# FoX attention in groups of two key tiles, with the first pair's operands read in two parts

## What is computed

```python
qa, ka, va, za, qf, kf, vf, zf, ff, ga, gf = jnp.split(u @ w_in[i], split_idx, axis=-1)
y_swa = _swa_branch(qa, ka, va, sinks[i]) * jax.nn.silu(za)     # 8 heads, window 128 + 16 meta keys, sink logit
log_f = jax.nn.log_sigmoid(ff + b_forget[i])
y_fox = _fox_branch(qf, kf, vf, log_f) * jax.nn.silu(zf)        # 8 heads, causal over all keys
merged = (jax.nn.sigmoid(ga + b_gate[i, 0]) * (y_swa @ w_up_swa[i])
          + jax.nn.sigmoid(gf + b_gate[i, 1]) * (y_fox @ w_up_fox[i]))
h = h + _rmsnorm(merged @ w_out[i], g_post[i])
# _fox_branch, per head: softmax(q k * scale + c_q - c_k, causal) @ v, with c = cumsum(log_f)
```

## Time and profile before

| what | us |
|---|---|
| median of 3 runs (lowest, highest) | 869.65 (867.27, 871.06) |
| the profiled execution, its own time | 866.6 |
| its span in the profile | 864.8 |
| first FoX tile to the start of the tile x = 8 of the last pair | 504.9 to 657.6 |
| from there to the first matmul of the fourth stage | 657.6 to 678.1 |
| the fourth stage | 678.1 to 864.8 |

### The profile page before, as it was taken

How to read it: one execution, slowest core, us unless ns; L and a number is a source line. 1 busy time by engine, 2 the same in 40 slices (tenths; PEclk the granted TensorE clock), 3 DMA queues, 4 the chain that set the end, 5 groups by cost and what they waited for, 6 DMA issues and landing times.

```text
span 864.8 us, 12858 instructions
## 1 busy us (share of the span) xinstructions
PE 809.0 (94%) x4514; PEld 651.2 (75%) x4514; DVE 500.1 (58%) x1050; ACT 314.6 (36%) x637; POOL 348.1 (40%) x284
## 2 busy tenths in 40 slices
PE   3999989999999999999999959998988799999996
PEld 3999989887878878878878746656654578878885
DVE  7934886357677686565564627676777434442112
ACT  6431241333333323333333236565667022232111
POOL 3412322444445444434444025655557244412221
PEclk9999999999999999999999979999999799999999
DMA  9331424569964626636635799946500645533221
GB/s 285 106 116 51 124 68 129 124 171 261 242 176 145 171 86 185 172 98 181 158 113 130 185 233 247 256 124 172 124 1 2 212 131 147 143 127 125 97 91 73
DMA packets 120879, 124.99 MB, mean 145 GB/s; under 512 B 29824, under 2 KB 91344, under 8 KB 120816
## 3 DMA queue, kind: packets, MB, share of 16 engines
q1 hardware_dynamic: 119376, 119.92, 50.9%
q10 hardware_dynamic: 1440, 4.26, 1.3%
HBM read 90.93 MB, written 34.92 MB: 146 GB/s over the span
## 4 chain that ended last, share of the span: by engine, by line
PE 76%; DVE 9%; issue 4%; SPq 3%; DMA 3%; POOL 2%; ACT 2%; DVEq 0%; ACTq 0%; POOLq 0%
PE PS L1827 18%; PE PS L1828 18%; PE PS L1829 18%; PE PS L2063 3%; PE PS L2065 3%; PE PS L2064 3%; PE PS L1924 2%; PE PS L1984 2%; DVE t_val L1579 2%; PE PS L1964 1%; SPq L871 1%; PE PS L1965 1%; PE PS L2003 1%; DMA QBs<-q_dram 1%; POOL acc L1199 1%
## 5 line engine op out<-in xcount | busy, mean ns | idle before, releaser
L1130 POOL TENSOR_TENSOR ops<-s_sum,ops 128x512 fp32r<-128x512 f32 x64 | 87.4, 1376 | 114.1 <-ACT ops L1228 114.1
L1827 PE MATMUL PS<-t_hi,ops 128*128 128x512 f32 x256 | 101.1, 395 | 0.0
L1828 PE MATMUL PS<-t_lo,ops 128*128 128x512 f32 x256 | 99.8, 390 | 0.0
L1829 PE MATMUL PS<-t_hi,ops 128*128 128x512 f32 x256 | 99.8, 390 | 0.0
L1130 POOL TENSOR_TENSOR ops<-raw,ops 128x512 fp32r<-128x512 f32 x48 | 65.0, 1354 | 70.0 <-ACT ops L1228 69.9
L1199 POOL TENSOR_TENSOR acc<-acc,p_fox 128x400 f32<-128x400 f32 (+5 forms) x76 | 61.5, 830 | 2.5 <-ACT p_fox L1352 0.9
L1151 POOL TENSOR_TENSOR w_plain<-raw,w_plain 128x1024 fp32r<-128x1024 f32 x10 | 28.0, 2801 | 85.0 <-ACT w_plain L1257 85.0
L1658 DVE TENSOR_TENSOR z_tmp<-u,PS 128x512 f32<-128x512 f32 x48 | 33.0, 687 | 48.9 <-PE PS L1829 28.1
L1352 ACT ACTIVATE p_fox<-PS,neg_c_col 128x512 f32<-128x512 f32 (+5 forms) x112 | 54.1, 532 | 17.2 <-PE PS L1970 14.4
L1228 ACT ACTIVATE ops<-s_sum 128x512 fp32r<-128x512 f32 x64 | 39.6, 624 | 54.9 <-DVE s_sum L1460 41.1
L1829 PEld LDWEIGHTS PS<-t_hi,ops 128*128 128x128 f32 x256 | 48.1, 188 | 10.6
(11 more groups left out here) (203 smaller groups left out, 2192.1 us busy)
## 6 DMA issues: line engine op xcount, KB each, us to landing
raw<-in_w_in_dram SPq DMA_DIRECT2D x34, 512.0 KB, 5.2
q_dram<-stage_b SPq DMA_DIRECT2D x32, 256.0 KB, 3.0
g_dram<-stage_b SPq DMA_DIRECT2D x32, 256.0 KB, 2.0
tanh_g<-g_dram SPq DMA_DIRECT2D x16, 512.0 KB, 3.9
max_k<-k_dram SPq DMA_DIRECT2D x16, 260.0 KB, 5.3
max_c<-neg_c_dram SPq DMA_DIRECT2D x8, 520.0 KB, 6.0
KA<-k_dram SPq DMA_DIRECT2D x8, 520.0 KB
x_all<-in_x_dram SPq DMA_DIRECT2D x8, 512.0 KB, 8.1
```

The lines of the kernel that those rows point to most:

```text
L1130: nc.gpsimd.tensor_tensor(ops[:, i % OPS, 1], op_source(p, name), ops[:, i % OPS, 0].bitcast(F32), ALU.subtract).then_inc(op_ready, 1)
L1827: pe.matmul(dst, hi_w, hi, start=first, stop=False)
L1828: pe.matmul(dst, hi_w, lo, start=False, stop=False)
L1829: return pe.matmul(dst, lo_w, hi, start=False, stop=last)
```

## The change

The list is made of 28 groups of two tiles. A group is: the two tile steps; `norm` of the items scored in the group ahead; `score` of this group's items (32 items over the first 24 groups: one, one, two, one, one, two, ...); the values of both tiles of the group ahead; `exp`; closing steps; `pv_swa` of the items transposed in the group ahead; `trans` of the items normalised in this one. `den` and the first two `rec` come two groups after the group of a block's last tile, the other two `rec` and `fin` one group later. `p_fox` gets 8 buffers, `probs` 4, `S_RING` stays 3. The loads of pair 0 are cut: 11 loads with values of key tiles 0 to 4, queries 0 to 511 and keys 0 to 639 count on `fox_first`, for which the first tile waits; 12 more with the rest are issued between them and those of `v_a`, `v_b`, and are waited for at (0, 1, 0).

```diff
-PT_RING = 6
+PT_RING = 8
 PSWA_RING = 2
-PROB_RING = 3
+PROB_RING = 4
 ...
-    spread = len(units) - 8
-    next_item, unnormed, normed, untransposed, unvalued = 0, None, None, None, None
+    groups = len(units) // 2
+    spread = groups - 4
+    scored, transposed = [], []
     closing = []
-    for u, (j, q, i) in enumerate(units):
-        first, last = i == 0, i == 4 * q + 4
-        x = u % per
-        steps.append(dict(kind="tile", j=j, q=q, i=i, u=u, first=first, last=last))
-        if j + 1 < PAIRS:
-            for turn, what in ((1, "load_queries"), (2, "load_z"), (3, "load_keys"), (5, "load_values")):
-                if x == turn:
-                    steps.append(dict(kind=what, j=j + 1, u=u))
-        if (j, x) in ((0, 7), (0, 9)):
-            steps.append(dict(kind="load_up", d=(x - 7) // 2, u=u))
-        untransposed, normed = normed, unnormed
-        if unnormed is not None:
-            steps.append(item("norm", unnormed))
-            unnormed = None
-        slot = next_item < ITEMS and (u + 1) * ITEMS // spread > u * ITEMS // spread
-        if slot:
-            steps.append(score(next_item))
-        if u:
-            pj, pq, pi = units[u - 1]
-            steps.append(dict(kind="values", j=pj, q=pq, i=pi, u=u - 1, first=pi == 0, last=pi == 4 * pq + 4))
-        if slot:
-            steps.append(item("exp", next_item))
-            unnormed = next_item
-            next_item += 1
-        if closing and closing[0][0] <= u:
-            steps += closing.pop(0)[1]
-        if unvalued is not None:
-            steps.append(item("pv_swa", unvalued))
-            unvalued = None
-        if untransposed is not None:
-            steps.append(trans(untransposed))
-            unvalued = untransposed
-        if last:
-            closing.append((u + 2, [dict(kind="den", j=j, q=q)]))
-            closing.append((u + 3, [dict(kind="rec", j=j, q=q, c=c) for c in range(2)]))
-            closing.append((u + 4, [dict(kind="rec", j=j, q=q, c=c) for c in (2, 3)] + [dict(kind="fin", j=j, q=q)]))
-        if j == PAIRS - 1:
-            turn = {1: 0, 3: 1, 5: 2, 7: PAIRS + 2, 9: PAIRS - 1, 10: PAIRS, 11: PAIRS + 1}
-            if x in turn:
-                steps.append(dict(kind="split_y", s=turn[x], c0=0, c1=2))
-            if x == 12:
-                steps.append(dict(kind="split_y", s=2 * PAIRS - 1, c0=0, c1=1))
-            if x == 4:
-                steps.append(dict(kind="split_up", d=0))
-            if x == 8:
-                steps.append(dict(kind="split_up", d=1))
+    for g in range(groups + 1):
+        now = range(2 * g, 2 * g + 2) if g < groups else ()
+        for u in now:
+            j, q, i = units[u]
+            x = u % per
+            steps.append(dict(kind="tile", j=j, q=q, i=i, u=u, first=i == 0, last=i == 4 * q + 4))
+            if j + 1 < PAIRS:
+                for turn, what in ((1, "load_queries"), (2, "load_z"), (3, "load_keys"), (5, "load_values")):
+                    if x == turn:
+                        steps.append(dict(kind=what, j=j + 1, u=u))
+            if (j, x) in ((0, 7), (0, 9)):
+                steps.append(dict(kind="load_up", d=(x - 7) // 2, u=u))
+        for n in scored:
+            steps.append(item("norm", n))
+        turned, scored = scored, []
+        if g < spread:
+            scored = list(range(g * ITEMS // spread, (g + 1) * ITEMS // spread))
+        for n in scored:
+            steps.append(score(n))
+        for u in range(2 * g - 2, 2 * g) if g else ():
+            j, q, i = units[u]
+            steps.append(dict(kind="values", j=j, q=q, i=i, u=u, first=i == 0, last=i == 4 * q + 4))
+        for n in scored:
+            steps.append(item("exp", n))
+        due = [x for x in closing if x[0] <= g]
+        closing = [x for x in closing if x[0] > g]
+        for _, extra in due:
+            steps += extra
+        for n in transposed:
+            steps.append(item("pv_swa", n))
+        for n in turned:
+            steps.append(trans(n))
+        transposed = turned
+        for u in now:
+            j, q, i = units[u]
+            x = u % per
+            if i == 4 * q + 4 and g < groups - 1:
+                closing.append((g + 2, [dict(kind="den", j=j, q=q)] + [dict(kind="rec", j=j, q=q, c=c)
+                                                                       for c in range(2)]))
+                closing.append((g + 3, [dict(kind="rec", j=j, q=q, c=c) for c in (2, 3)] +
+                                [dict(kind="fin", j=j, q=q)]))
+            if j == PAIRS - 1:
+                turn = {1: 0, 3: 1, 5: 2, 7: PAIRS + 2, 9: PAIRS - 1, 10: PAIRS, 11: PAIRS + 1}
+                if x in turn:
+                    steps.append(dict(kind="split_y", s=turn[x], c0=0, c1=2))
 ...
+    steps += [dict(kind="den", j=j, q=q)] + [dict(kind="rec", j=j, q=q, c=c) for c in range(4)]
+    steps.append(dict(kind="fin", j=j, q=q))
 ...
                     elif (p, name) == (N_COUPLES - 1, "S2"):
                         sp.wait_ge(product_done, i + 1)
-                        load_values(sp, 0)
+                        load_values(sp, 0, fox_first, 0, 5)
                     elif (p, name) == (N_COUPLES - 1, "S1"):
                         sp.wait_ge(product_done, i + 1)
                         sp.wait_ge(halves_ready[0], 2)
                         sp.wait_ge(max_stored, 16 * PAIRS)
-                        load_queries_fox(sp, 0)
+                        load_queries_fox(sp, 0, fox_first, 0, 4)
                     elif (p, name) == (N_COUPLES - 1, "A12"):
-                        load_keys_fox(sp, 0)
+                        load_keys_fox(sp, 0, fox_first, 0, 5 * P)
+                        load_keys_fox(sp, 0, fox_loaded[0], 5 * P, LENGTH)
+                        load_queries_fox(sp, 0, fox_loaded[0], 4, NQ)
+                        load_values(sp, 0, fox_loaded[0], 5, NK)
                         sp.dma_start(v_a[0:A_ROWS, 0, :], vd[0, 0:A_ROWS]).then_inc(swa_loaded, 16)
 ...
-                    if i == 0 and q == 0:
+                    if (j, q, i) == (0, 0, 0):
+                        pe.wait_ge(fox_first, 16 * FIRST_LOADS)
+                        pe.wait_ge(halves_cleared, 3)
+                    elif i == 0 and q == (0 if j else 1):
                         pe.wait_ge(fox_loaded[j], 16 * FOX_LOADS)
 ...
-                                        p_fox[0:keys, x % PT_RING, 0:w], start=st["first"], stop=st["last"])
+                                        p_fox[x % PT_RING][0:keys, 0:w], start=st["first"], stop=st["last"])
```

More of the change, by code:

```diff
@@ L288, in attention_steps @@
     j, q, i = units[-1]
-    steps.append(dict(kind="values", j=j, q=q, i=i, u=len(units) - 1, first=False, last=True))
-    for _, extra in closing:
-        steps += extra
+    steps += [dict(kind="den", j=j, q=q)] + [dict(kind="rec", j=j, q=q, c=c) for c in range(4)]
+    steps.append(dict(kind="fin", j=j, q=q))
     steps.append(dict(kind="split_y", s=2 * PAIRS - 1, c0=1, c1=2))
-    assert next_item == ITEMS and unvalued is None and unnormed is None and untransposed is None and normed is None
+    assert not closing and not scored and not transposed
@@ L442, in build @@
         VF[1] = sb("VF1", [P, NK, P], on=ph2)
-        p_fox = sb("p_fox", [P, PT_RING, BANK], on=ph2)
+        p_fox = [sb(f"p_fox{n}", [P, BANK], on=ph2) for n in range(6)]
         sb("gap", [P, 64], on=ph2)
@@ L843, in natural, with load_queries_fox @@
             return PS[:, 2 * (n % 4):2 * (n % 4) + 2, :].rearrange("p a b -> p (a b)")
-        def load_queries_fox(queue, j):
-            n, done = j % 2, fox_loaded[j]
-            q_hi, q_lo = (qd[PAIRS + j, x] for x in range(2))
+        def load_queries_fox(queue, j, done, t0, t1):
+            n, cols = j % 2, slice(P * t0, P * t1)
+            q_hi, q_lo = (qd[PAIRS + j, x][:, cols] for x in range(2))
             for half in (Q0, Q1):
-                queue.dma_start(QA[n][half].bitcast(F32),
+                queue.dma_start(QA[n][half, :, cols].bitcast(F32),
@@ L858, in load_keys_fox @@
-        def load_keys_fox(queue, j):
-            n, done = j % 2, fox_loaded[j]
-            k_hi, k_lo = (kd[1 + j, x] for x in range(2))
+                queue.dma_start(QB[n][row:row + 1, h, cols].bitcast(F32),
+                                max_dram[2 * j + h, t0:t1].rearrange("(o t) q -> o (t q)", o=1)).then_inc(done, 16)
+        def load_keys_fox(queue, j, done, c0, c1):
+            n, cols = j % 2, slice(c0, c1)
+            k_hi, k_lo = (kd[1 + j, x][:, cols] for x in range(2))
             for half, src in ((Q0, k_hi), (Q1, k_lo)):
-                queue.dma_start(KA[n][half].bitcast(F32),
+                queue.dma_start(KA[n][half, :, cols].bitcast(F32),
@@ L1190, in _ @@
                         dst = acc[0:keys, f % 2, h, c0:c0 + w]
-                        tile = p_fox[0:keys, n % PT_RING, 0:w]
+                        tile = p_fox[n % PT_RING][0:keys, 0:w]
                         pool.wait_ge(fox_exp, n + 1)
```

44 lines of the change are left out of this document (27 added, 17 removed).

## The result

| what | before | after |
|---|---|---|
| median (lowest, highest), us | 870.36 (867.27, 872.48), 4 runs | 895.29 (893.75, 896.32), 4 runs |
| ratio, 95% interval | | 1.0288 [1.0252, 1.0324] |
| profiled execution, own time | 866.6 | 895.7 |
| span in the profile | 864.8 | 893.9 |
| first SWA `score` | 508.9 | 508.2 |

The change costs 25 us, where +8.7 us was forecast (877 named, range to 890): the sign was right and the time lies outside the range. In the two profiled executions the difference is 29.1 us, because the profiled one before lies 3.8 us under its median; attention alone has it all.

The account below looks back on a forecast made before the run. TensorE's own work plus short waits was taken to bound attention, with GpSimd setting its end. Terms -8.0 - 11.8 + 5.4 + 14.4 + 3.9 + 0.7 + 1.3 - 0.9 + 3.7 = +8.7 us; named 877, range 862 to 890.

Parts of the forecast that it names:

- the largest term: In double groups the second pv_swa waits for VectorE's y step behind closing steps: +14.4 us, bounds 4.6 and 27.
- VectorE keeps up: Rival: closings spread enough, each double pv_swa costs only 0.65 us, no lag, no end delay; 861 us, chance 0.27.
- the start: Cut loads start tiles 0 and 1 near 498, first score still at 508; 0.8 gained, +1.5 slow clock: net +0.7 us.
- the end: Last pair from tile x = 8: -0.9 us at its start, then late up_hi delays GpSimd's sums, +3.7 us.
- The slow-clock stretches are taken as many as before: Assumption in the sum: no more stretches at the 1.2 GHz level than before the change.
- a rival (+4 to 5): "More slow clock": two or three more slow stretches after long waits, 2 us lost each; 882 us, no separate chance.
- The exps: Fourth score of a group waits for the first exp, late on the diagonal behind masks: +5.4 us, bounds 0 and 7.2.
- Unmasked tiles have time enough: Within the exps term: three scores take 1.4 us, the exp is done about 1.3 us after the start.
- Switches: Fewer passages between full-width and 64-column products on TensorE, 0.32 us each: -8.0 us, bounds 0 and 9.
- The page's rule: Packing speeds TensorE but not PSUM emptying; if that held throughout, no switch saving and total +16.7; busy times judged against it.
- Lag passed on: After fin VectorE ends late, next group's norm is late and trans waits: +3.9 us, bounds 0 and 8.
- the queries of pair 1: First item's queries land at 542.3 under a full DMA; TensorE comes earlier and waits: +1.3 us.

Follow-up runs that it names:

- the fills: Changed kernel with thrown-away products after the first pv_swa of groups 4, 16, 19, 22, 25: ten each 892.5 us, as many as fit 888.6 us.
- the two small edits: On the back to back kernel: each head's mask right behind its scores, 871.03 us; split_up(1) at x = 6 in place of 8, 871.76 us.
- back to back: Changed kernel with both pv_swa of a group written into two halves of their bank, VectorE reading both after the second: 872.96 us, ratio 1.0017.
- the best kernel: Back to back plus masks by head, split_up(1) at x = 6, and norm and score between a group's two tile steps: 860.95 us, ratio 0.9877.

## Why the prediction was wrong in size

**Right: the mechanism of the largest term, and its places.** I forecast waits for `y` in groups 4, 7, 10, 13, 16, 19 and 22 of 2.4, 0.65, 0.65, 0.65, 3.5, 3.9 and 2.6 us. They are 3.46, 0.64, 0.55, 1.08, 4.00, 4.82 and 2.42: 17.0 where the sum had 14.4. The run without this wait (22 us back) and the one that only moves `pv_swa` ahead of the closings (15 us) show it to be the cause, and the rival "VectorE keeps up" is out.

**Right: the start.** First tile 498, first `score` 508, and no gain from the cut. Timeline of PE after:

```profile
498.20 0.77 PE L1981 MATMUL PS<-QA,KA 128*128 128x512 f32 x1 [2.69 <-DMA KB<-k_dram]
...
508.17 0.54 PE L1958 MATMUL PS<-kk_s,QAs 128*128 128x208 f32 x1 [5.75 <-DMA v_b<-v_dram]
```

**Right: the end.** Timeline of ACT, POOL and PE after; tile x = 8 of the last pair starts at 682.05:

```profile
688.11 1.05 ACT L1247 ACTIVATE up_hi<-up_raw 128x1024 fp32r<-128x1024 f32 x1
689.23 2.35 POOL L1150 TENSOR_TENSOR up_lo<-up_raw,up_hi 128x1024 fp32r<-128x1024 f32 x1 [4.88 <-ACT up_hi L1247]
...
703.85 1.97 PE L2011 MATMUL PS<-acc,ones 128*64 128x512 f32 x4 [5.02 <-POOL acc L1213]
```

`up_hi` comes 6.1 us behind that tile (forecast 5.65, before 1.9) and the tail is 24.8 us (forecast 20.5 + 3.7 = 24.2). Nearly all of the miss lies ahead: the tile was expected at 662.6 and came 19.5 us later.

**The step that failed most: "The slow-clock stretches are taken as many as before".** They doubled, from 20.3 to 43.7 us in attention. A stretch at the low level costs at most half its length, so 23.4 us more of it are up to 11.7 us; the fills show 6.7 us, net of the waits that then grow. I had the row that says so the earlier trace rows and the arithmetic in a rival (+4 to 5), which was also too small: I gave each stretch 4 us, where behind the waits of groups 19 and 22 the low level lasted 10.2 and 6.8 us. Some 10 of the 43.7 us stand at the start, from 508 to 518, for which the sum had its +1.5 us; the other 14 more are the groups'. I should have put it in the sum, since the same text had named the waits that bring it.

**The exps, a term mis-sized: +5.4 us.** The idle time for them is 11.3 us in 16 waits, so about +6 more. The forecast counted on masks that delay the first exp on the diagonal. But the four longest waits, 6.8 of the 11.3 us, end with a first exp that ScalarE began late because other steps stood ahead of it. The two longest, and what ScalarE did ahead of them:

```profile
585.16 0.39 PE L1981 MATMUL PS<-QA,KA 128*128 128x272 f32 x1 [1.79 <-ACT p_fox L1366]
...
677.37 0.50 PE L1981 MATMUL PS<-QA,KA 128*128 128x512 f32 x1 [2.36 <-ACT p_fox L1366]
```

```profile
581.65 0.69 ACT L1366 ACTIVATE p_fox<-PS,neg_c_col 128x512 f32<-128x512 f32 x1 [3.25 <-DVE acc L1763]
...
674.75 1.04 ACT L1247 ACTIVATE up_hi<-up_raw 128x1024 fp32r<-128x1024 f32 x1
675.70 1.04 ACT L1403 ACTIVATE y_hi<-y 128x1024 fp32r<-128x1024 f32 x1
```

At 581.65 an exp had waited 3.25 us for one of VectorE's adds to `acc`; four SWA exps and the `den` copy followed, and the first exp of the new group began only at 584.5. At 674.7 `up_hi` and `y_hi` stood ahead of the exps, in an unmasked group. The other two (1.40 and 1.22 us) ended behind SWA exps that had waited for `neg_max`, and behind `y_hi`. So ScalarE itself came late, behind other steps of its queue and behind VectorE, which the forecast's sum for the exps did not look at.

"Unmasked tiles have time enough" is wrong too. Timeline of PE after, an unmasked tile, and below it the waits of the weight load, 508 to 700 us, after and before:

```profile
523.40 0.40 PE L1981 MATMUL PS<-QA,KA 128*128 128x512 f32 x1
523.64 0.40 PE L1982 MATMUL PS<-QB,KB 128*128 128x512 f32 x1
524.15 0.50 PE L1981 MATMUL PS<-QA,KA 128*128 128x512 f32 x1
```

```profile
PEld PS L1981 <- ACT p_fox L1366: 18.4, 26, 2.8
```

```profile
PEld PS L1964 <- ACT p_fox L1352: 6.9, 11, 1.4
```

The second tile's second head starts 0.51 us after the matmul ahead of it, where others start 0.23 apart. A matmul's duration of 0.40 covers the gap, so it counts as hardly idle: only the weight load, which waits for the same bank, shows it, 26 times against 11. Such a 0.28 us in a group eats most of the 0.32 us that the group saves by its one passage the less. The runs fit this: with `y` out of the way the groups gave nothing (+1.6 us), and with the exps given time, and the two small edits, the kernel came to -10.5.

**Switches, -8.0 us.** Shown in one place only. Timeline of PE after:

```profile
530.41 1.94 PE L2001 MATMUL PS<-p_fox,VF 128*64 128x512 f32 x8
532.18 1.03 PE L2011 MATMUL PS<-acc,ones 128*64 128x512 f32 x4
```

The values of two tiles hold TensorE 1.77 us, where two steps apart hold 1.01 each. For the whole stage it can be read roughly, by counting each us at the low level as half: TensorE's busy time is then 150.8 - 10.2 = 140.6 us before and 159.3 - 21.9 = 137.4 after, and 137.4 again back to back. So the matmuls hold TensorE some 3 us less, give or take the 2 us of the clock's rounding, and not 8; the waits hidden under durations are in this figure. The page's rule that I set against it (the Trainium skill, TensorEngine Tiling (Array Packing), PSUM Bottleneck) spoke of the emptying of PSUM as the limit: here ScalarE is busy for 105 of 198.8 us, so not on the mean, but a bank that an exp had not emptied held up the weight load 26 times between 508 and 700 us. Weighing it by mean busy shares was the wrong test; with three banks for four scores the test is the time of the first exp.

**Lag passed on, +3.9, and the queries of pair 1, +1.3.** Both were too high for this kernel. The lag was to show as `trans` waiting for `probs`: that is 1.1 us in 4 waits. VectorE's lateness came out elsewhere, as in the exp at 581.65. And TensorE has no wait for `QBs` in the trace of the kernel after; with the cut loads alone it is 2.3 us and in the best kernel 2.6, where it was 0.9 before.

**By size.** Of 29.1 us between the profiles, 8.7 were forecast: the waits for `y` are 2.6 us over the forecast's to group 22, the exps about 6, and the low clock up to 11.7. These come to 20.2 of the 20.4 us missed, but that is partly luck: they leave out the switches (some 5 us less saved than forecast), and against them the lag (2.8 us less), the queries (1.3 less) and the 1.5 us of low clock that the start already had in the sum. And the last of the three is an upper bound. So the agreement proves no more than that these are large enough.

## What to carry to other kernels

When steps are merged into groups, ask for each shared buffer how many of its users now stand in one group, and what is ahead of the step that frees it on the freeing engine; then either give the two users room side by side in the same bank, or give the freeing step the first place. Put other work between the producer's last free bank and its next use: the same operations in another order were worth 10 us here. Put a term for the slow clock behind each new long wait into the sum: here four of the five had 3.4 to 10 us of it, and the fifth had none. Follow the queue of the engine that empties a bank back to what it waits for itself. And look at the weight load's waits too, since a wait shorter than a matmul's duration does not appear as idle time.

## What I had not expected

Five waits of 2.35 to 4.8 us, filled with thrown-away products, give 6.7 us back although TensorE does more work; filled in part (ten products each) they give 2.8 us, which the intervals can't tell from nothing. But 52 such products in the long waits of the start gave nothing that can be told: a wait of 2.15 us right behind brought the low clock again. And closing steps behind `pv_swa`, worth 15 us where its bank was waited for, cost 6 us when put behind `trans` as well, in a kernel where it wasn't.

Left open: what the reordering would give in single units, without the groups, and how much of the exps' lateness comes from VectorE's adds to `acc`, which no run moved by themselves.
